# A third copy of gate_up, 156 tokens wide, in the expert loop of a retention, attention and MoE layer

## What is computed

```python
def expert_block(args):
    xb, e = args
    gu = xb @ w_gate_up[e] + b_gate_up[e]
    gate = jnp.minimum(gu[:, 0::2], SWIGLU_LIMIT)
    up = jnp.clip(gu[:, 1::2], -SWIGLU_LIMIT, SWIGLU_LIMIT)
    hidden = (up + 1.0) * gate * jax.nn.sigmoid(SWIGLU_ALPHA * gate)
    return hidden @ w_down[e] + b_down[e]
```

## Time and profile before

| | |
|---|---|
| median of 3 runs (lowest, highest) | 2222.38 us (2222.38, 2222.68) |
| the profiled execution | 2220.2 us |
| its span, first to last instruction | 2218.3 us |
| TensorE busy with matmuls | 2134.1 us, 96% of the span |
| VectorE, ScalarE, GpSimd busy | 1282.0, 765.1, 330.6 us |
| mean granted TensorE clock | 0.984 of full speed |
| mean DMA traffic | 230 GB/s |

### The profile page before, as it was taken

The page is one execution under the profiler, slowest core; times in us unless marked ns, Lnnn a source line. Parts: engine busy times, 40 slices in busy tenths (PEclk is TensorE's granted clock), DMA queues, the critical chain, the costliest instruction groups (busy, mean ns, idle before and its releaser), DMA issues.

```text
span 2218.3 us, 41969 instructions
## 1 busy us (share of the span) xinstructions
PE 2134.1 (96%) x16349; PEld 1916.6 (86%) x16350; DVE 1282.0 (58%) x2579; ACT 765.1 (34%) x1360; POOL 330.6 (15%) x237
## 2 busy tenths in 40 slices
PE   6999999899968999999999999999999999999996
PEld 5988888777857899899989999999999999999996
DVE  6434534787457556456665555665566665576654
ACT  3243134477213332223333333332333332333332
POOL 1100200200000121111211211211121211212121
PEclk9999999999978999999999999999999999999998
DMA  4231221303364788778988887897898897999983
GB/s 164 88 99 64 77 95 58 115 1 124 130 222 173 256 296 295 241 268 308 331 304 274 293 305 267 307 332 264 274 314 308 309 327 255 307 318 332 320 282 92
DMA packets 257635, 509.55 MB, mean 230 GB/s; under 512 B 7450, under 2 KB 44366, under 8 KB 257294
## 3 DMA queue, kind: packets, MB, share of 16 engines
q1 hardware_dynamic: 234268, 451.96, 57.3%
q0 software_dynamic: 21968, 51.67, 9.5%
q10 hardware_dynamic: 1344, 5.14, 0.7%
HBM read 473.09 MB, written 33.55 MB: 228 GB/s over the span
## 4 chain that ended last, share of the span: by engine, by line
PE 94%; DVE 2%; issue 2%; DMA 1%; ACT 0%; POOL 0%; ACTq 0%; SPq 0%; DVEq 0%; POOLq 0%
PE bank L1119 45%; PE bank L1099 16%; PE bank L860 13%; PE bank L1107 3%; PE bank L958 2%; PE bank L971 2%; PE bank L1060 1%; PE bank L1005 1%; PE bank L1007 1%; PE bank L1006 1%; PE bank L1053 1%; PE bank L942 1%; PE bank L1064 1%; PE bank L1084 1%; PE bank L1026 1%
## 5 line engine op out<-in xcount | busy, mean ns | idle before, releaser
L1119 PE MATMUL bank<-hx,ring 128*128 128x140 f32 (+1 forms) x8192 | 1021.8, 287 | 2.5 <-DVE hx L1571 1.7
L1119 PEld LDWEIGHTS bank<-hx,ring 128*128 128x128 f32 x8192 | 1014.7, 197 | 5.7 <-DVE hx L1571 1.9
L1099 PE MATMUL bank<-work_r,hx_r 128*128 128x512 f32 x1024 | 337.1, 411 | 0.0
L1553 DVE TENSOR_TENSOR mix_r<-ring,work_r 128x1024 fp32r<-128x1024 f32 x256 | 305.1, 1223 | 41.1 <-ACT work_r L792 41.0
L809 ACT ACTIVATE hx<-hx 128x168 f32<-128x168 f32 x256 | 87.9, 343 | 583.1 <-DVE hx L1569 582.1
L1569 DVE TENSOR_SCALAR hx<-bank,small 128x168 f32<-128x168 f32 x256 | 100.3, 392 | 274.7 <-PE bank L1119 274.5
L792 ACT ACTIVATE work_r<-ring 128x1024 fp32r<-128x1024 f32 x256 | 257.7, 1042 | 0.0
L1099 PEld LDWEIGHTS bank<-work_r,hx_r 128*128 128x128 f32 x1024 | 189.4, 190 | 44.2 <-issue 10.5
L1099 PE MATMUL bank<-mix_r,hx_r 128*128 128x512 f32 x512 | 201.0, 393 | 0.0
L800 ACT ACTIVATE hx<-bank,small 128x512 f32<-128x512 f32 x64 | 44.0, 688 | 321.6 <-PE bank L1064 175.0
L603 POOL DMA_INDIRECT out_x<-hx,small x32 | 51.9, 1622 | 665.6 <-ACT hx L802 646.5
(11 more groups left out here) (220 smaller groups left out, 2326.9 us busy)
## 6 DMA issues: line engine op xcount, KB each, us to landing
ring<-in_w_gate_up SPq DMA_DIRECT2D x128, 2048.0 KB, 12.9
ring<-in_w_down SPq DMA_DIRECT2D x64, 2048.0 KB, 13.0
mix<-in_w_in SPq DMA_DIRECT2D x14, 1024.0 KB, 5.0
work<-in_w_in SPq DMA_DIRECT2D x14, 1024.0 KB, 5.0
ring<-in_x SPq DMA_DIRECT2D x8, 512.0 KB, 8.9
hx<-in_w_out SPq DMA_DIRECT2D x1, 4096.0 KB, 14.1
work<-in_x ACTq DMA_DIRECT2D x8, 512.0 KB, 4.7
out_x<-work SPq DMA_DIRECT2D x8, 512.0 KB, 4.4
```

Of the source, the lines that this page charges most:

```text
L1099: mm = e.matmul(bank[2 + t][:, :], h[:, k], w[:, t, k], start=False, stop=k == KD - 1 and w is dn_lo, skip_group_check=True)
L1119: mm = e.matmul(bank[f % 2][:, part * CAP:part * CAP + w], gu_ring[:, k, f * 256 + part:(f + 1) * 256:2], xT[:, k, 0:w], start=k == 0, sto ...
L1553: e.tensor_tensor(dn_lo[:, nh, k:k + 2], dn_ring[:, k:k + 2, nh * CH:(nh + 1) * CH], dn_hi[:, nh, k:k + 2].bitcast(F32), ALU.subtract).the ...
```

## The change

One number is added to the table of widths:

```diff
-WIDTHS = (140, CAP)
+WIDTHS = (140, 156, CAP)
```

## The result

The changed kernel takes **2272.11 us** (median of 4 runs, 2270.68 to 2274.68) against 2222.38 us before: a ratio of **1.0229** (95% interval 1.0211 to 1.0247), slower by 50 us. The profiled execution took 2272.72 us with a span of 2270.8 us, 52.5 us above the span of before. The side that was forecast is right, and 2272 lies in the range; the forecast number, 2438 us, is far off.

The account below looks back on a forecast made before the run. PE was taken to bound the kernel. From the profiled 2220.2 us, less 10.2 saved, plus 226 for 32 missing pages, came 2436, and 2438 us with the median 2.2 above that execution; range 2235 to 2580.

Parts of the forecast that it names:

- What bounds the kernel: Expert loop: PE busy 96% of the span, so a microsecond of PE's time in a block is one of the kernel.
- The saving: Four wide blocks run `gate_up` at 156 columns instead of 168: 2.56 us a block, 10.2 us together.
- The loop outgrows the store, which ends at eight pages: PE's loop grows from 6.1 to 8.4 pages of instructions; the store was taken to keep no more than 8.
- How often a page is missing: Place by address: branch back misses in blocks 1 to 31, block 4 adds one; 32 misses, 226 us in all.
- some 130 loads: Sign in the profile: q8's code loads instead of 40, four a block between 760 and 2190 us.
- The price of one: A missing page at a branch costs 7.06 us, read from the first block's jump; 3 to 11 us allowed.
- Rival 2: Eight places, by order of loading or of use; only wide blocks push pages out: 2283 or 2240 us; chance 0.19.
- order of use: Rival 2's second form, pages replaced by use: 4 misses, +18, 2240 us; chance 0.19 for both forms together.
- The side and the range: Whole kernel: slower at 0.81, range 2235 to 2580 us; the forecast's own range 2308 to 2564.
- Rival 1: The store keeps ten pages or more, only the saving is left, q8 stays silent: 2212 us; chance 0.17.
- Rival 3: The store is one window of neighbouring pages emptied by jumps out of it; two misses a block: 2650 us; chance 0.06.
- Rival 4: The new copy changes nothing, since blocks of 51 us wait for weights; chance 0.01.

Follow-up runs that it names:

- e2: Kernel before, plus 24 matmuls that never run (97 instructions) between the copies of `gate_up` and `down`: 2227.64 us, 1.0020 times before.
- e3: Kernel before, plus 48 matmuls that never run (193 instructions) between the copies of `gate_up` and `down`: 2777.91 us, 1.2493 times before.
- e7: The same instructions as e6, but PE's loop begins at slot 64 of its page: 2580.85 us, 1.1609 times the kernel before.
- e6: Kernel before with `gate_up` in two halves, `token_list` once between, a 156 copy in the first half only, loop on a page boundary: 2213.34 us, 0.9957.
- e4: The changed kernel with a hint for the loop's branch back: 2219.94 us, 0.9985 times the kernel before.
- e12: The changed kernel with PE's loop at slot 224 of its page instead of 75: 2686.65 us, 1.2082 times the kernel before.

## Why the prediction was right and wrong

- *What bounds the kernel*: right. PE is still 95% busy, the added time is PE's own idle time and clock. One reading was off: PE's slices are at 9 throughout from the fourteenth on, not from the tenth (the twelfth and thirteenth are at 6 and 8); nothing hangs on it.
- *The saving*: right. 10.2 us forecast, 9.9 measured (17.04 us for half a `gate_up`, 16.96 forecast). It is real and more than paid back.
- *The loop outgrows the store, which ends at eight pages*: right. The trace before showed only that eight are held. e2, e3 and e7 put the end between the eighth page and the ninth. The Trainium skill (Runtime: NRT & Kernel Launch, Instruction fetch mechanics) has 128 KiB in 16 KiB blocks, eight blocks, which agrees; e6 and e7 add that what counts is the pages touched, not the 2048 instructions: both have 1785.
- *How often a page is missing*: **this step failed.** "If a page's place in the store follows from its address, the ninth page takes the place of the first" led to 32 missing pages. A page's place follows from the order of loading. After the first block the seven pages of the path of 140 stand in the ring together, with `down`'s behind the copy's as if the skipped ones did not exist, and only a block that runs another copy pushes them out. 11 pages are missing, not 32, and 85 loads are made. (The forecast's own sign, "some 130 loads", did not follow from its "four a block": 31 x 4 and the 40 of before are 164.)
- *The price of one*: 7.06 us forecast, (52.5 + 9.9) / 11 = 5.7 measured. The waits for a single page at a block's top are 2.8 to 3.2 us, not 4.4. The DMA engines are less busy there, with a share of 0.57 from 1006 to 1009 us, before the top of block 6, against 1.01 from 707.1 to 711.7 us in the kernel before; that this makes the wait shorter fits, but was not tested. The prediction named this pull and left it out of the sum.
- *Rival 2, the order of loading*: the mechanism that happened, at 0.19. It gave 10 missing pages in blocks 4, 5, 14, 18 and 25 and 2283 us, 11 us too high by the price. The count was one short (block 6), as it let `down`'s pages survive block 4; of each pair it put the jump to `down` a block late. Its other form, order of use, with 4 missing pages and 2240 us, falls. What the profile already held against an address-given place was little, and I should have let both stand nearly even rather than 3 to 1.
- *The side and the range*: slower is right for the reason given, a loop that outgrows eight pages. That 2272 lies in 2235 to 2580 is not the forecast's doing: its own range, 2308 to 2564, does not hold it, and the part below was there for rival 2.
- *Rivals 1, 3 and 4*: q8 isn't silent, blocks of 140 don't stall, and the copy is faster where it runs; all three fall.
- *Left open*: what the hint does to the order of the places. Worked through, the ring rule with the branch's page put in place of the next one gives 20 loads in the loop for e4, not 13. e12's six loads above the rule are not explained either.

## What to carry to other kernels

Before a copy of an inner body is added to a loop, count the loop's instructions on the engine that runs it and place them in pages: here 97 more instructions cost next to nothing and 193 cost 25%, as the loop with the page ahead went from eight pages to nine, while 574 cost only 2%. The loads on the instruction queue inside the loop tell it at a glance, zero or not. Where a body is over the edge, a hint for the branch back (52 us in e4) or another start slot (368 us from e7 to e6) is worth more than the 10 us that the copy was meant to save, and a measured "slower" says nothing of the idea itself until the loads of code are looked at.

## What was not expected of the hardware

- A third of the code cost ten times as much: 193 instructions 555 us, 574 instructions 50 us. By the ring rule each block of the padded loop needs nine pages in turn and throws out what it needs next; in the larger loop a block of 140 jumps over whole pages, needs seven and settles.
- The start of a loop within its page is worth 470 us in the kernel before (slot 75: 2222 us, slot 236: 2693 us).
- A branch hint that names only the branch back also spared the jumps forward over the copies, and cost nothing where the loop fits.
- A float32 matmul record with its weight load hardly gets shorter below 140 columns: 119.1 ns at 140, 117.7 at 128, where 168 to 140 took off 23.4.
